# First delta head of each layer: decay columns and exponential moved into the third projection, and the instructions around the spreading reordered

## What is computed

```python
gc = jnp.cumsum(g, axis=-1)
decay = jnp.where(incl, jnp.exp(jnp.where(incl, gc_i - gc_j, 0.0)), 0.0)
lower = jnp.where(strict, (k * beta) @ k.T * decay, 0.0)
u, w  = triangular_solve(lower + I, [v * beta, k * beta * exp(gc)])
a_intra = jnp.where(incl, q @ k.T * decay, 0.0)
# scan over chunks:
v_new = u_i - w_i @ s
o_i   = q_dec @ s + a_i @ v_new
s     = s * g_last + k_dec.T @ v_new
# then: o = rmsnorm(o_f + reversed o_b) ; y = o * silu(z)
```

## Time and profile before

| | |
|---|---|
| median of 3 runs | 2433.28 us (2432.92 to 2435.49) |
| the profiled execution | 2435.23 us |
| its span, first to last instruction | 2433.7 us |
| mean granted clock of TensorE | 0.991 |
| PE, PEld busy | 2339.8 us (96%), 2240.2 us (92%) |
| DVE, ACT, POOL busy | 1356.0, 1029.4, 288.8 us |
| mixer A, layer 0 | about 59.8 to 334.3 us of the span |
| mixer A, layer 1 | about 1259.1 to 1537.9 us |

### The profile page before, as it was taken

How to read it: one execution, slowest core, us unless ns; L and a number is a source line. 1 busy time by engine, 2 the same in 40 slices (tenths; PEclk the granted TensorE clock), 3 DMA queues, 4 the chain that set the end, 5 groups by cost and what they waited for, 6 DMA issues and landing times.

```text
span 2433.7 us, 49251 instructions
## 1 busy us (share of the span) xinstructions
PE 2339.8 (96%) x19072; PEld 2240.2 (92%) x19072; DVE 1356.0 (56%) x2569; ACT 1029.4 (42%) x2212; POOL 288.8 (12%) x422
## 2 busy tenths in 40 slices
PE   6899899999999999999999998999999999999998
PEld 5888889999999999989988888999999999999898
DVE  5677754776333435663566776457753334356543
ACT  4776532332245324542357664233322443254422
POOL 1222210000111001110012221200000120111000
PEclk9999999999999999999999999999999999999999
DMA  6111232111343233214221111421132342222222
GB/s 263 51 45 45 62 105 88 53 45 53 127 97 94 81 104 94 68 57 153 82 76 43 45 48 57 138 70 45 36 89 70 85 103 71 81 68 75 86 73 87
DMA packets 63263, 195.45 MB, mean 80 GB/s; under 512 B 16376, under 2 KB 16542, under 8 KB 62928
## 3 DMA queue, kind: packets, MB, share of 16 engines
q1 hardware_dynamic: 46880, 148.55, 18.4%
q0 software_dynamic: 16176, 44.07, 7.2%
HBM read 177.97 MB, written 8.39 MB: 77 GB/s over the span
## 4 chain that ended last, share of the span: by engine, by line
PE 80%; DVEq 5%; DVE 5%; issue 3%; ACT 3%; DMA 2%; SPq 1%; POOL 0%; ACTq 0%; POOLq 0%
PE proj L805 50%; PE mix L805 26%; DVEq L2360 5%; PE mix L808 4%; DMA area<-raw 1%; DMA raw<-in_w_mod 1%; DVE area L2349 1%; DVE w_lo L2349 1%; DVE raw L2349 0%; ACT area L1781 0%; ACT w_hi L1666 0%; DVE merged L2349 0%; SPq L291 0%; ACT merged L1827 0%; ACT L1762 0%
## 5 line engine op out<-in xcount | busy, mean ns | idle before, releaser
L805 PE MATMUL proj<-h_hi,w_hi 128*128 128x320 f32 x3072 | 739.7, 321 | 9.2 <-issue 4.6
L805 PE MATMUL proj<-h_lo,w_hi 128*128 128x320 f32 x3072 | 704.4, 310 | 0.0
L805 PE MATMUL proj<-h_hi,w_lo 128*128 128x320 f32 x3072 | 701.3, 310 | 0.0
L2349 DVE TENSOR_TENSOR w_lo<-raw,w_hi 128x1024 fp32r<-128x1024 f32 x232 | 283.4, 1222 | 455.7 <-ACT w_hi L1666 454.8
L805 PEld LDWEIGHTS proj<-h_hi,w_hi 128*128 128x128 f32 x3072 | 506.5, 189 | 22.8 <-issue 10.0
L805 PEld LDWEIGHTS proj<-h_lo,w_hi 128*128 128x128 f32 x3072 | 517.3, 189 | 0.0
L805 PEld LDWEIGHTS proj<-h_hi,w_lo 128*128 128x128 f32 x3072 | 515.4, 189 | 0.0
L1666 ACT ACTIVATE w_hi<-raw 128x1024 fp32r<-128x1024 f32 x232 | 246.0, 1060 | 532.6 <-PE proj L805 329.9
L805 PE MATMUL mix<-area 128*128 128x128 f32 (+8 forms) x4576 | 387.3, 260 | 25.2 <-DVE area L2572 14.6
L805 PEld LDWEIGHTS mix<-area 128*128 128x128 f32 (+5 forms) x4576 | 328.2, 156 | 66.6 <-issue 20.2
L1666 ACT ACTIVATE area<-mix 128x384 f32<-128x384 f32 (+8 forms) x394 | 158.1, 420 | 502.5 <-PE mix L805 397.5
(11 more groups left out here) (325 smaller groups left out, 2708.7 us busy)
## 6 DMA issues: line engine op xcount, KB each, us to landing
raw<-in_w_in SPq DMA_DIRECT2D x128, 512.0 KB, 3.5
raw<-in_w_mb SPq DMA_DIRECT2D x96, 512.0 KB, 3.5
raw<-in_w_mod POOLq DMA_DIRECT2D x32, 512.0 KB, 4.4
area<-in_bias POOLq DMA_DIRECT2D x64, 128.0 KB, 4.9
raw<-in_w_out SPq DMA_DIRECT2D x16, 512.0 KB, 3.5
out_x<-area SPq DMA_DIRECT2D x10, 512.0 KB, 2.6
merged<-in_w_mod SPq DMA_DIRECT2D x8, 512.0 KB, 11.1
area<-area POOLq DMA_DIRECT2D x64, 64.0 KB, 2.0
```

What stands on the lines that cost most here:

```text
L805: return T.matmul(out, l, r, start=start, stop=stop)
L2349: return V.tensor_tensor(out, a_, b_, op)
```

## The change

No arithmetic is added or taken away; instructions are moved, and the waits that the new order needs are changed.

- **First head, before the levels.** PE: units 0 to 2 of the front go to the start of the third projection (block 2) instead of behind it, and wait for `ab_v` (the cumulated decays) instead of `ab_done`; units 3 to 6 stand together behind the first eighth of block 3, unit 7 behind the second, 8 and 9 two eighths later. The first head gets banks of its own. ACT: columns and exponential come ahead of SiLU (in layer 1 SiLU stays where it was), `A_take(0, 2)` behind unit 7, `A_hi(6)` ahead of units 8 and 9. DVE: `A_decays(0)` right behind `A_lo(3)`, and `A_convolve(0, 2)` behind `A_blocks(0)`.
- **Around the spreading.** PE: units 1 and 2 of the next head's front stand among the eighths ahead of `A_level_q`. ACT: they are taken out ahead of `A_spread`; `A_keys(h, kd, 3, 0)` comes ahead of `A_level`, `A_mid` ahead of `A_hi(4h+8)`; `A_recall` of the next head is earlier; `A_values` is split into three parts.
- **Masks.** For heads 0 to 2 POOL's `A_masked(h)` waits for `A_decays(h+1)` on DVE instead of the spreading, DVE does `A_decays(h+1)` right behind `update(h)`, and POOL's order is masks, then `A_o_root(h-1)`. For head 3 the wait is as before and only this order changes.

```diff
-FRONT_BANK = (1, 3, 1, 1, 3, 1, 2, 1, 0, 1)
+FRONT_BANK = ((1, 3, 0, 2, 1, 3, 0, 2, 1, 3),) + ((1, 3, 1, 1, 3, 1, 2, 1, 0, 1),) * (HEADS - 1)
...
                 def A_masked(h):
                     decT = decTs[h % 2]
-                    pool.wait_ge(A_x.sem, A_x.at(layer, 5 * h + 1))
+                    if h == HEADS - 1:
+                        pool.wait_ge(A_x.sem, A_x.at(layer, 5 * h + 1))
+                    else:
+                        pool.wait_ge(A_own.sem, A_own.at(layer, 4 * h + 5))
...
+                    A_masked(h)
                     if h:
                         A_o_root(h - 1)
-                    A_masked(h)
...
-                        pe.wait_ge(ab_done.sem, ab_done.at(layer, 1))
+                        pe.wait_ge(ab_v.sem, ab_v.at(layer, 3))
...
-                        fill(h, 0, 6)
+                        fill(h, 0, 2)
+                        pe.wait_ge(A_su.sem, A_su.at(layer, 5 * h))
+                        A_front(h + 1, 1)
+                        fill(h, 2, 3)
+                        A_front(h + 1, 2)
+                        fill(h, 3, 6)
                         A_level_q(h)
-                        A_front(h + 1, 1)
-                        A_front(h + 1, 2)
...
                 else:
-                    unit(0, 0, 2)
-                A_front(0, 0)
-                A_front(0, 1)
-                eighths(0, 3, 0, 2)
-                A_front(0, 2)
-                for u in range(3, 8):
+                    eighths(0, 2, 0, 2)
+                for u in range(3):
                     A_front(0, u)
-                    eighths(0, 3, u - 1, u)
-                eighths(0, 3, 7, 14)
+                if layer == 0:
+                    eighths(0, 2, 2, 8)
+                eighths(0, 3, 0, 1)
+                for u in range(3, 7):
+                    A_front(0, u)
+                eighths(0, 3, 1, 2)
+                A_front(0, 7)
+                eighths(0, 3, 2, 16)
                 for u in (8, 9):
                     A_front(0, u)
-                    eighths(0, 3, u + 6, u + 7)
-                eighths(0, 3, 16, 24)
+                    eighths(0, 3, u + 8, u + 9)
+                eighths(0, 3, 18, 24)
...
-                A_values(h)
+                A_values(h, (0, 3) if more else range(TILES))
...
+                        if more and n in (0, 3):
+                            A_values(h, (1, 2) if n == 0 else (4,))
...
                 A_lo(3)
+                A_decays(0)
+                A_lo(4)
+                A_factor(0)
+                A_blocks(0)
                 A_convolve(0, 2)
-                A_factor(0)
-                A_lo(4)
-                A_decays(0)
-                A_blocks(0)
                 A_lower(0)
...
                     update(h)
+                    if more:
+                        A_decays(h + 1)
                     if h:
                         A_out_squares(h - 1)
                     update_mid(h)
                     if h:
                         A_out_normed(h - 1)
                     if more:
-                        A_decays(h + 1)
                         A_lo(4 * h + 8)
```

More of the change, by code:

```diff
@@ L474, in relay_in @@
                 def relay_in(h):
-                    sp.wait_ge(A_own.sem, A_own.at(layer, 3 * h + 2))
+                    sp.wait_ge(A_own.sem, A_own.at(layer, 4 * h + 3))
                     held(sp)
@@ L481, in relay_out @@
                 def relay_out(h):
-                    sp.wait_ge(A_own.sem, A_own.at(layer, 3 * h + 3))
+                    sp.wait_ge(A_own.sem, A_own.at(layer, 4 * h + 4))
                     held(sp)
@@ L616, in A_front @@
                     pt(A_head(5, h), A_head(5, h), both(rn_k_sq(h))).then_inc(A_rn.sem, A_rn.step)
-                    pool.wait_ge(A_own.sem, A_own.at(layer, 3 * h + 2))
+                    pool.wait_ge(A_own.sem, A_own.at(layer, 4 * h + 3))
                     held(pool)
@@ L655, in _ @@
                 for h in range(HEADS):
-                    pool.wait_ge(A_own.sem, A_own.at(layer, 3 * h + 3))
+                    pool.wait_ge(A_own.sem, A_own.at(layer, 4 * h + 4))
                     held(pool)
@@ L999, in A_front @@
                 def A_front(h, u):
-                    o = lambda c, n=128: M[:, 512 * FRONT_BANK[u] + 128 * c:512 * FRONT_BANK[u] + 128 * c + n]
+                    o = lambda c, n=128: M[:, 512 * FRONT_BANK[h][u] + 128 * c:512 * FRONT_BANK[h][u] + 128 * c + n]
                     if u == 0 and h == 0:
                         pe.wait_ge(merged_step.sem, merged_step.at(layer, 0))
-                        pe.wait_ge(ab_done.sem, ab_done.at(layer, 1))
-                    if u in FRONT_BEFORE and FRONT * h + FRONT_BEFORE[u] >= 0:
-                        pe.wait_ge(A_fev.sem, A_fev.at(layer, FRONT * h + FRONT_BEFORE[u] + 1))
+                        pe.wait_ge(ab_v.sem, ab_v.at(layer, 3))
+                    if u in FRONT_BEFORE[h]:
+                        pe.wait_ge(A_fev.sem, A_fev.at(layer, FRONT * h + FRONT_BEFORE[h][u] + 1))
                     if h:
@@ L1815, in A_front @@
                     else:
+                        A.drain()
                         last = copy(A_tmv[:, 9:10, :], src(1))
@@ L1832, in A_recall, with A_values @@
                         A_keys(h, Rk, 5, d)
-                def A_values(h):
+                def A_values(h, ts):
                     for d in range(2):
-                        for t in range(TILES):
+                        for t in ts:
                             A.activation(Rv[:, d, t, :], A_tmv[:, TILES + t, :], ACT.Identity, scale=beta_rn[h % 2][:, d, t:t + 1])
@@ L1840, in A_gram_rows @@
                     if d == 0:
-                        act.wait_ge(A_own.sem, A_own.at(layer, 3 * h + 1))
+                        act.wait_ge(A_own.sem, A_own.at(layer, 4 * h + 2))
                         A.drain()
@@ L1887, in join_gate @@
                     elif g == 0:
-                        act.wait_ge(A_own.sem, A_own.at(layer, 3 * HEADS - 1))
+                        act.wait_ge(A_own.sem, A_own.at(layer, 4 * HEADS - 1))
                     elif g == 1:
@@ L1919, in _ @@
                     A_hi(3)
-                    A_silu(0)
-                A_take(0, 2)
                 for u in range(3):
                     A_front(0, u)
-                for u in range(3, 6):
+                A_exp(0)
+                if layer == 0:
+                    A_silu(0)
+                A_hi(4)
+                for u in range(3, 8):
                     A_front(0, u)
-                A_hi(4)
-                A_exp(0)
-                for u in (6, 7):
-                    A_front(0, u)
+                A_take(0, 2)
                 A_gram_rows(0, 0)
@@ L1934, in _ @@
                 A_gate(0)
+                A_hi(6)
                 for u in (8, 9):
@@ L1945, in _ @@
                     more = h < HEADS - 1
+                    act.wait_ge(A_sb.sem, A_sb.at(layer, 5 * h))
+                    A_keys(h, kd, 3, 0)
                     A_level(h)
                     if more:
-                        A_front(h + 1, 1)
-                        A_front(h + 1, 2)
                         A_exp(h + 1)
+                        A_silu(h + 1)
                     else:
                         join_gate(0)
-                    act.wait_ge(A_sb.sem, A_sb.at(layer, 5 * h))
-                    A_keys(h, kd, 3, 0)
+                    A_mid(h)
                     if more:
-                        A_silu(h + 1)
                         A_hi(4 * h + 8)
-                    A_mid(h)
-                    if not more:
+                    else:
                         join_gate(1)
@@ L2525, in A_decays @@
                     for c, w in QUARTERS:
-                        mul(D32[c], decTs[h % 2][c, :, :, c], lower_16[c].unsqueeze(1).unsqueeze(1).to_broadcast([32, 2, TILES, 32]))
+                        last = mul(D32[c], decTs[h % 2][c, :, :, c], lower_16[c].unsqueeze(1).unsqueeze(1).to_broadcast([32, 2, TILES, 32]))
+                    last.then_inc(A_own.sem, A_own.step)
                 def A_factor(h):
```

18 lines of the change are left out of this document (10 added, 8 removed).

## The result

The changed kernel takes **2398.99 us** (median of 4 runs, 2396.22 to 2402.2) against 2433.1 for the kernel before: a ratio of 0.9861, 95% interval 0.9843 to 0.9879. The forecast was 2406.2, with 2398 to 2421 as its range. The direction held; the gain was 34 us where 27.1 were worked out. So the time lies 7 us under the forecast, outside its own range of 2401 to 2412, and only 1 us inside the wide one; what came is the rival "No new slow stretch, short new waits" (2399.5, chance 0.14). The profiled execution took 2400.28 us, with a span of 2398.7 (35.0 less than before) and a mean granted clock of 0.998 (0.991 before).

What follows compares the result with a forecast made beforehand. PE, busy 96% of the span, bounds the kernel, so time comes only from its idling or low clock. Terms 4.0 + 3.0 + 3.7 + 4.5 + 11.9 + 7.8 - 4.4 - 3.4 = 27.1 off 2433.3 give 2406.2 us; range 2398 to 2421.

Steps and rivals of the forecast that it cites:

- No new slow stretch, short new waits: Rival: no new slow stretches, short new waits, and the spreading's stretch at head 2 goes too; 2399.5 us, chance 0.14.
- First heads, 4.0 + 3.0: First head: the ACT and DVE chain brings the scaling 4.0 us earlier in layer 0, 3.0 in layer 1.
- From there to the spreading nothing changes: First head, layer 0: from DVE's scaling to the spreading all stays the same, so the 4.0 us gain holds.
- Units ahead of the level, 3.7: Heads 0 to 2, both layers: six transposes per head move inside PE's wait for the spreading, saving 3.7 us.
- POOL at head 0, 4.5: Head 0: masks no longer delay block 7's weights; waits of 2.1 and 0.7 us and one 1.7 us slow stretch go.
- The mid level, 11.9: Mixer A: PE's waits for ACT's copies go, 6.8 us, with three slow stretches behind them, 5.1 us.
- Head 3, 7.8: Head 3, both layers: the norming is unheld, so the 2.2 us output wait and a slow stretch behind each go.
- A new wait ... taken as 1.1, in four places: minus 4.4: Heads 1 and 2, both layers: PE newly waits 0.7 to 1.6 us for the normed output, costing 4.4 us.
- Does the clock drop behind it? ... I take two of four: minus 3.4: Heads 1 and 2: two of the four new output waits bring a slow stretch, costing 3.4 us; ends 0 and 6.8.
- Masks held longer: Rival: DVE's squares hold the masks, so four output waits grow by 2.2 us and slow the clock; 2418.4 us, chance 0.15.
- DVE paces the head: Rival: PE's gains in the levels are waited out at the next spreading; 2416.6 us, chance 0.13.
- chains do not shorten: Rival, first heads: PE or the relay holds the scaling, so 7.0 us less is gained; 2413.2 us, chance 0.10.

Runs made afterwards that it cites:

- e2: Changed kernel with the order around the spreading undone on PE and ACT; 2416.4 us.
- e4: Changed kernel with ACT's scalings of the values in one piece again, ahead of the scan's first copy; 2398.61 us.
- e9: Kernel before with the new order around the spreading alone, values in one piece; 2424.28 us.
- e6: Changed kernel with POOL taking the root ahead of the masks again at head 3 alone; 2407.42 us.
- e8: Changed kernel with DVE's low weights of block 3 in layer 1 moved ahead of the product that waits for ACT's exponential; 2399.34 us.
- e12: Changed kernel with POOL taking the root ahead of the masks at heads 1 and 2 alone; 2402.24 us.
- e7: Changed kernel with one eighth of a block moved ahead of the first level at heads 0 to 2, both layers; 2395.1 us.
- e5: Kernel before with the part for the masks alone; 2426.58 us.
- e10: Kernel before with the new order at the first head alone; 2423.05 us.
- e3: Changed kernel with the masks part undone: masks at the spreading for every head, root first, next decays behind the norming; 2416.67 us.

## Why the prediction was right, and where it fell short

**First heads, 4.0 + 3.0: right.** The scaling starts at 84.08 us, 83.8 was worked out; the opening was 1.2 us later, so up to there the chain gained 4.9 us, not 4.0. "From there to the spreading nothing changes" did not quite hold: DVE waits 2.46 us for the inverses to come back by DMA, 1.86 before, and 4.2 us reach the level. DVE in layer 0: blocks, convolution, weights, scaling:

```profile
76.60 1.98 DVE L2361 TENSOR_TENSOR area<-area,gate_sg 32x320 f32<-32x320 f32 x4 [0.66 <-ACT gate_sg L1674]
...
79.71 0.89 DVE L2520 SCALAR_TENSOR_TENSOR area<-area,small 128x641 f32<-128x641 f32 x1
...
82.95 1.22 DVE L2361 TENSOR_TENSOR w_lo<-raw,w_hi 128x1024 fp32r<-128x1024 f32 x1
84.08 1.30 DVE L2361 TENSOR_TENSOR raw<-raw 40x256 f32<-40x256 f32 x3
```

The table load weighed against a rule sits between two activations without a gap: exponential 66.36 to 67.63, load at 67.66 for 1.28, SiLU at 68.95. So the switch cost 1.3 us.

The 2.66 us that the Trainium skill, "ScalarE: Activation LUTs", "What ACT_TABLE_LOAD costs", gives with a drain does not occur here.

**Units ahead of the level, 3.7: right or better.** The six waits for the spreading at heads 0 to 2 fell by 0.6, 0.4, 0.8, 2.3, 1.0 and 0.65 us, 5.8 in all; how much of that is the six transposes alone was not tried apart from ACT's order. In e2 most of it came back (10.0 us in the six, 5.5 in the changed kernel, 11.2 before). Such waits also differ without a change of order: e4's six are 3.2 us.

**POOL at head 0, 4.5: right.** The first level is at 102.28, that is 101.1 without the later opening, with a wait of 1.36 (1.4 forecast); the convolution behind it takes 0.89, and nothing waits before block 7.

**The mid level, 11.9: right in what it removes, wrong as a part on its own.** No wait is left there. But e9 shows that without the masks part 5.6 of these 11.9 us come back as waits for DVE. And the 5.1 us in it for three slow stretches were one execution's draw: behind these waits one began in 12 of 17 cases over four kernels. The sum was right since both parts were in it; the working did not see that one needed the other. The missing row was in the trace of before: decays of four operations that take 2.00 us at the first head took 4.7 us at head 1 of the kernel before,

```profile
179.55 4.71 DVE L2349 TENSOR_TENSOR area<-area,blocks 32x320 f32<-32x320 f32 x4
```

beside the second mask, and the forecast looked for holds at heads 0 and 3 only.

**Head 3, 7.8: right in size** (e6: 8.4). The waits of 2.2 us are gone in both layers; that both had a slow stretch behind them was chance, in the other profiles it was 4 of 8.

**"A new wait ... taken as 1.1, in four places: minus 4.4": mis-sized.** It measured 0.38 in each, 1.5 in all. PE's transposes at head 1:

```profile
175.57 0.74 PE L811 MATMUL proj<-ident,merged 128*128 128x128 f32 x5 [0.38 <-DVE merged L2361]
```

DVE and POOL at that place:

```profile
163.99 1.97 DVE L2361 TENSOR_TENSOR area<-area,blocks 32x320 f32<-32x320 f32 x4
166.04 0.82 DVE L2361 TENSOR_TENSOR tmp<-merged 128x640 f32<-128x640 f32 x1
166.94 0.82 DVE L2648 TENSOR_REDUCE stat<-tmp 128x5 f32<-128x640 f32 x1
167.84 1.85 DVE L2361 TENSOR_TENSOR stat<-stat 128x5 f32<-128x5 f32 x1
...
174.60 0.82 DVE L2361 TENSOR_TENSOR merged<-merged,stat 128x640 f32<-128x640 f32 x1 [3.44 <-POOL stat L591]
```

```profile
166.14 3.53 POOL L591 TENSOR_TENSOR area<-area,tri 128x1280 f32<-128x1280 f32 x1 [11.82 <-DVE area L2361]
170.15 2.91 POOL L591 TENSOR_TENSOR area<-area 128x1280 f32<-128x1280 f32 x1 [0.48 <-DVE stat L2652]
173.01 1.20 POOL L640 TENSOR_TENSOR stat<-stat,neg_half 128x5 f32<-128x5 f32 x1
```

The chain from the end of `update` (164.1) to the end of the norming (175.4) is 11.3 us, where 11.0 and 0.1 to 0.7 for a hold were added up. PE's side was wrong. The prediction took 0.6 us for units 1 and 2 off the time in which PE comes to the transposes. Before, those units stood between the level and `update`; from `update` on nothing of them was left to take off. From `update` to the transposes PE had 14.2 us before, and less 1.6 and 1.7 that is 10.9; it came 11.1 us behind `update`. With the 0.6 left in, the same sum gives a wait of 0.1 to 1.0 us.

**"Does the clock drop behind it? ... I take two of four: minus 3.4": wrong.** None of the four. Two more slow stretches left mixer A that no term had, behind the waits for the spreading at head 2 of layer 0 and head 0 of layer 1 (1.89 and 3.44 us before), besides the one in the front of layer 0, counted at nothing. The prediction foretold six or seven instead of ten; one is left, behind the 2.03 us in layer 1, and by e8 and e12 it costs nothing that can be seen.

The three together are 2.9 + 3.4 + 3.4 = 9.7 us, against 9.1 us by which the stretches of the table beat their terms (36.2 - 27.1). That they match so closely is partly luck, since the terms for the spreading and the slow stretches vary by more than the 0.6 us between executions.

**Rivals.** "No new slow stretch, short new waits", at 2399.5, is what happened. "Masks held longer": the first mask was held, at 3.53 us, and held a 0.17 us operation for 1.7, but it did not have to let the squares pass: mask and squares' last product ended together (169.67 and 169.69 us), and both masks took 6.9 us where 6.4 were added up. "DVE paces the head" fell with e2 and e7, "chains do not shorten" with the timeline, and the decays did not wait for ACT's exponential at any of the heads 1 to 3: they start 0.1 us before the last row of `update` has ended.

## What to carry over

Undo and add each part: here the parts alone gave 24 us, the whole 34, and the last part to be added looked worth 17, for the larger part because two engines were late for PE at nearly the same place and the first wait hid the second. Before pricing a wait that goes, read whether another engine is also late there. When a wait is worked out as a difference of two arrivals, count both from the same event, and take from it only what stands behind that event. And an operation that takes twice its usual time in the timeline is a price tag: look for its neighbour on the other engine at every place, not where the wait is longest.

## What was not expected of the hardware

**POOL and DVE.** With both inputs in SBUF, a DVE operation that starts beside a mask on POOL is held until the mask has ended, and then takes its usual time less 0.1 to 0.2 us. Its end came 0.68 us after the mask's for the norming (0.82 unheld), 1.08 for low weights (1.22) and 0.02 for 128x5 elements (0.17). So: norming 0.82 to 3.36 or 3.52 us, low weights 1.22 to 3.92, decays 1.97 to 4.7, each operation of the convolution 0.89 to 3.38, and one on 128x5 elements 0.17 to 1.85. The reduction beside the mask took its usual 0.82, and so did copies out of PSUM (mid level, 1.31 to 1.32 in each kernel). The Trainium skill, "SBUF — State Buffer", "Who interferes with whom", says that a DVE instruction with two SBUF inputs contends with a GpSimd one that reads SBUF, and that reductions never contend; the trace agrees. That even a tiny operation is held until the mask ends was the surprise; what helped was to put the masks beside operations of which few have two such inputs.

**The clock.** Which wait a slow stretch follows depends on its length, on its place and on chance. In the profiled executions of before, e2, e5 and e10, PE waits 1.58 to 1.61 us for the mid level 17 times; a stretch of 3.4 us at 0.50 began behind 12 of them. Behind the output's 2.2 us at head 3 it was 6 of 10 (before, e3, e6, e9, e10). Behind 12 waits of 1.2 to 1.4 us for `A_out` (e3, e9, e12) there was none, and none behind the 0.38 us waits. At the first level of a head the same lengths read otherwise: of 25 waits of 1.5 to 1.75 us for the spreading (all fourteen profiles) one was followed by a stretch, of 15 waits of 2.0 to 4.2 us eleven were, the stretch beginning at most 0.8 us before the wait's end or 2 us behind it. Two windows behind such waits at head 1, e5 (1.60 us):

```profile
177.70:181.10 3.40, 3.40 (x15) 3.36 (x15) 1.86 (x6) 1.93 (x9) 2.92 (x2) 0.50 0.02 5
```

and e12 (1.21 us):

```profile
177.80:181.20 3.40, 3.40 (x27) 3.40 (x28) 3.10 (x8) 0.53 (x1) 1.28 (x4) 1.00 0.00 0
```

So a stretch's 1.7 us belongs to a wait of 1.6 us about two times in three at the mid level and almost never at the first level, and no wait under 1.5 us had one. What makes the difference between the two places was not tried. Such chance is part of why executions of one kernel differ: the slowest of the changed kernel's four, 2402.2 us, has a mean clock of 0.995, the other three 0.998. What decides in the single case stays open.
